# First block of a two-block transformer: output product, second norm, up and down products joined into one stage

## The reference, cut to what matters

```
mixed = sigmoid(g_ssm) * (y_ssm @ w_ssm_out) + sigmoid(g_att) * (y_att @ w_att_out)
h = h + mixed @ w_o                                   # output product, 1024 -> 1024
hn = rmsnorm(h, norm2_g)                              # second norm
a, b = hn @ w_up[:, :2816], hn @ w_up[:, 2816:]       # up product
c = a[t-2]*conv_w[0] + a[t-1]*conv_w[1] + a[t]*conv_w[2] + conv_b   # along the sequence
h = h + (gelu(c) * b) @ w_down                        # down product, 2816 -> 1024
return h[16:528]                                      # 512 tokens go on to the second block
```

## Time and profile before

| | us |
|---|---|
| median of the runs | 2160.52 |
| lowest and highest of 3 | 2160.28, 2163.2 |
| span of the profiled execution | 2159.5 |
| busy TensorE, VectorE, ScalarE in it | 1979.5, 1357.7, 955.4 |

### The profile page before, as it was taken

How to read it: one execution, slowest core, us unless ns; L and a number is a source line. 1 busy time by engine, 2 the same in 40 slices (tenths; PEclk the granted TensorE clock), 3 DMA queues, 4 the chain that set the end, 5 groups by cost and what they waited for, 6 DMA issues and landing times. The chain is left out here.

```text
span 2159.5 us, 29553 instructions
## 1 busy us (share of the span) xinstructions
PE 1979.5 (92%) x11864; PEld 1644.8 (76%) x11864; DVE 1357.7 (63%) x1895; ACT 955.4 (44%) x1409; POOL 163.7 (8%) x209
## 2 busy tenths in 40 slices
PE   5998997997999989899997999978998999799996
PEld 5888887996899978687675888866786667688884
DVE  7874543726455454443346999975526783799996
ACT  5562434402111000252445777752224884677773
POOL 3443000000000000000010200020000000110010
PEclk9999998997999999999998999997997999899998
DMA  7434111314223122232141999971531001299993
GB/s 218 103 82 111 61 40 59 116 45 88 97 79 110 67 78 80 84 98 78 40 147 53 361 401 396 377 269 35 156 114 51 21 21 59 89 382 400 385 384 139
DMA packets 176327, 322.37 MB, mean 149 GB/s; under 512 B 46736, under 2 KB 112976, under 8 KB 176192
## 3 DMA queue, kind: packets, MB, share of 16 engines
q1 hardware_dynamic: 148464, 282.92, 37.5%
q0 software_dynamic: 11488, 31.28, 4.5%
q10 hardware_dynamic: 16240, 6.29, 1.1%
HBM read 299.41 MB, written 17.89 MB: 147 GB/s over the span
## 5 line engine op out<-in xcount | busy, mean ns | idle before, releaser
L2318 PE MATMUL ps<-m_ws,m_xbT 128*128 128x512 f32 x1344 | 314.5, 390 | 0.0
L2318 PEld LDWEIGHTS ps<-m_ws,m_xbT 128*128 128x128 f32 x1344 | 251.9, 188 | 52.1
L2545 DVE TENSOR_TENSOR m_ws<-ring,m_ws 128x2048 fp32r<-128x2048 f32 x112 | 256.0, 2289 | 15.8 <-ACT m_ws L2394 14.3
L1648 PE MATMUL ps<-ffT,ff_ws 128*128 128x264 f32 (+1 forms) x1056 | 241.6, 324 | 4.4 <-DVE ff_ws L433 4.4
L2394 ACT CAST m_ws<-ring 128x2048 fp32r<-128x2048 f32 x112 | 212.9, 1907 | 42.4 <-PE ps L2360 24.8
L1648 PEld LDWEIGHTS ps<-ffT,ff_ws 128*128 128x128 f32 x1056 | 176.8, 190 | 20.2 <-DVE ff_ws L433 4.5
L1648 PE MATMUL ps<-ffT_lo,ff_ws 128*128 128x264 f32 (+1 forms) x528 | 170.3, 322 | 0.0
L2360 PE MATMUL ps<-m_ws,m_hT 128*128 128x512 f32 x672 | 167.3, 398 | 0.0
L2542 DVE TENSOR_TENSOR m_ws<-ring,m_ws 128x2048 fp32r<-128x2048 f32 x56 | 128.2, 2290 | 24.8 <-ACT m_ws L2392 24.8
L2360 PEld LDWEIGHTS ps<-m_ws,m_hT 128*128 128x128 f32 x672 | 122.2, 188 | 23.6
L2392 ACT CAST m_ws<-ring 128x2048 fp32r<-128x2048 f32 x56 | 107.0, 1910 | 51.4 <-PE ps L2318 30.7
(11 more groups left out here) (548 smaller groups left out, 4078.8 us busy)
## 6 DMA issues: line engine op xcount, KB each, us to landing
ring<-in_moe_w_gate SPq DMA_DIRECT2D x112, 512.0 KB, 5.7
ring<-in_moe_w_up SPq DMA_DIRECT2D x112, 512.0 KB, 8.1
ring<-in_moe_w_down SPq DMA_DIRECT2D x56, 1024.0 KB, 8.4
ring<-in_w_up SPq DMA_DIRECT2D x22, 1024.0 KB, 5.2
ring<-in_w_in SPq DMA_DIRECT2D x16, 1024.0 KB, 6.9
ring<-in_gla_w_in SPq DMA_DIRECT2D x12, 1024.0 KB, 5.3
ring<-in_w_down SPq DMA_DIRECT2D x11, 1024.0 KB, 4.8
ring<-in_nsa_w_in SPq DMA_DIRECT2D x10, 1024.0 KB, 11.0
```

The lines of the kernel that those rows point to most:

```text
L1648: ins = nc.tensor.matmul(ps[:, bank, 0:b - a], w[j][:, k, s * P:(s + 1) * P], x[l][:, k, a:b], start=(k == 0 and j == l), stop=(k == KD - ...
L2318: ins = nc.tensor.matmul(ps[:, it % 2, :], xbT[:, blk % 2, a, 4 * half + k, :].bitcast(F32R), v[b][:, k, :], start=(half == 0 and k == 0 a ...
L2545: ins = V.tensor_tensor(o, x.rearrange("p (j k w) -> p j k w", k=4, j=2), x0, ALU.subtract)
```

## The change

The five stages become one, `mix_stage`. The split of weight slabs there is done by `Split` throughout, ScalarE rounding and VectorE subtracting; `Split` now gets a list of places ("homes") and of the event that frees each, in place of a fixed number of buffers.

- **Output product by token tile.** For each of the five token tiles, the 16 learned tokens first, all four weight slabs are used in turn, so the four slabs have to stay resident (two of them in the memory of `qkT` and `gT`). A tile is finished after 4 x 24 matmuls. VectorE adds it at once to its row of `h`, ScalarE squares it, takes its own logarithm and exponential, VectorE scales it, and TensorE transposes it in the middle of the following tile's product (`turn_y`); the last tile is turned within the first up products.
- **Up product.** The `a` halves have 258 columns in place of 264 (the first 12 learned tokens aren't needed by the convolution). The first two turns are rearranged so that products on the first tiles run while the last tile is being normed. Each turn has a ScalarE rounding of a slab in place of the VectorE one.
- **Down product.** The first input pair is split while the up product still runs. The last two slabs are done by token tile: all 24 matmuls of a tile, then the next tile; a finished tile is added to `h` and transposed (`turn_x`) during the next tile's matmuls. The high and low parts go to buffers (`xT_hi`, `xT_lo`) that the GLA stage reads, and the stage `x0` is gone.
- **Loads.** The norm's and the convolution's weights are loaded by POOL after the reload of `x`, in place of ScalarE's queue at the start of two stages.

The core of the diff (lines that are only "..." leave parts out):

```diff
@@ output product, TensorE
-                for j in range(4):
-                    w = S.both(pe, 21 + j, slab_view(KD, 256))
-                    for b, (n, c0, t) in enumerate(KT):
-                        x = 5 * j + b
...
+                for x, (n, c0, t) in enumerate(KT):
+                    if x >= 2:
+                        pe.wait_ge(h_added, x - 1)
+                    for j in range(4):
+                        w = S.both(pe, 21 + j, slab_view(KD, 256))
...
+                        if j == 1 and x:
+                            turn_y(x - 1)
@@ second norm, ScalarE, for each tile
+                for x, (n, c0, t) in enumerate(KT):
+                    act.wait_ge(h_added, x + 1)
+                    if x >= 2:
+                        act.wait_ge(turned, 2 * (x - 1))
+                    link(nc.scalar.activation(y2[0:n, x % 2, :], h[0:n, t, :], ACT.Square, accum_out=st[0:n, 0, x:x + 1]))
+                    link(nc.scalar.activation(st[0:n, 1, x:x + 1], st[0:n, 0, x:x + 1], ACT.Ln, bias=eps[0:n], scale=1 / D))
+                    nc.scalar.activation(st[0:n, 2, x:x + 1], st[0:n, 1, x:x + 1], ACT.Exp, scale=-0.5).then_inc(rs, 1)
+                    for hf in range(2):
+                        act.wait_ge(turned, 2 * x + hf + 1)
+                        nc.scalar.copy(hT[:, 4 * hf:4 * hf + 4, c0:c0 + n].bitcast(F32R), turn_bank(x, hf, n)).then_inc(xt_hi, 1)
+                    if x == 3:
+                        F.hi(act, 1)
+                        F.hi(act, 2)
@@ up product, TensorE
+                up(0, 0, 2, 0, A_HALVES[0])
+                pe.wait_ge(h_added, NK)
+                up(0, 1, 0, 0, A_HALVES[0])
+                pe.wait_ge(xt_lo, 8)
+                up(1, 0, 6, 0, B_HALVES[0])
+                turn_y(NK - 1)
+                up(1, 1, 7, 0, B_HALVES[0])
+                pe.wait_ge(xt_lo, 10)
...
+                for i in range(2, FT):
+                    s = i % 2
+                    pe.wait_ge(a_out, i - 1)
+                    up(i // 2 * 2, s, 2 - 2 * s, 0, A_HALVES[0])
+                    up(i // 2 * 2, s, 3 - 2 * s, 0, A_HALVES[1], a_done)
+                    pe.wait_ge(g_done, i - 1)
+                    up(i // 2 * 2 + 1, s, 6 + s, 0, (META, T1), b_done)
@@ up product, VectorE (ScalarE's turns: copy of a, gelu, F.hi)
+                for it in range(FT + 1):
+                    if it:
+                        F.lo(dve, it + 2)
...
+                        V.tensor_tensor(glu(i)[:, 0], ge[:, i % 2], ps[:, 6 + i % 2, :], ALU.mult).then_inc(g_done, 1)
+                    if it == FT - 1:
+                        down_x(0)
@@ down product, TensorE
+                for i in range(ND - 2):
+                    for kk in range(2):
+                        for t in range(TT):
+                            if i == 0 and kk == 0 and t:
+                                pe.wait_ge(*((a_out, FT - 1), (a_out, FT), (g_done, FT))[t - 1])
+                            ins = down(i, kk, t)
+                    ins.then_inc(dn_read, 1)
+                for t in range(TT):
+                    for i in range(ND - 2, ND):
+                        for kk in range(2):
+                            ins = down(i, kk, t)
+                    ins.then_inc(y_done, 1)
+                    if t:
+                        turn_x(t - 1)
+                turn_x(TT - 1)
@@ second block
-                self.norm_stage("x0", TILES2, h, None, m["xh"], None, None, None, 0.0, dstT_lo=m["xl"])
```

More of the change, by code:

```diff
@@ L360, in weight_order @@
         self.n_moe.append(self.moe_slabs(1))
-    def fm_product(self, slab, kt, w, col, rhs, spans, done, m=P):
-        v = slab_view(kt, w)(self.W.slot(slab))
-        for bank, a, b in spans:
-            for k in range(kt):
-                ins = self.nc.tensor.matmul(self.ps[0:m, bank, 0:b - a], v[:, k, col:col + m], rhs(k, a, b),
-                                            start=(k == 0), stop=(k == kt - 1))
-        ins.then_inc(done, 1)
-        return ins
     def fm_product3(self, w, col, x, out, done, m=P):
@@ L508, in _ @@
-                if dstT is None:
-                    return
-                for i, (r, t, c0) in enumerate(tiles):
+                for t in range(TT if dstT is not None else 0):
                     for hf in range(2):
-                        act.wait_ge(turned, 2 * i + hf + 1)
-                        to = dstT[:, 4 * hf:4 * hf + 4, c0:c0 + r]
-                        nc.scalar.copy(to if dstT_lo is None else to.bitcast(F32R), banks(2 * i + hf, r)).then_inc(evac, 1)
+                        act.wait_ge(turned, 2 * t + hf + 1)
+                        nc.scalar.copy(dstT[:, 4 * hf:4 * hf + 4, P * t:P * (t + 1)].bitcast(F32R), bank(t, hf)).then_inc(evac, 1)
@@ L1499, in _, with up @@
                                                        start=(k == 0 and wa == xa), stop=(k == KD - 1 and xa == 1))
-                        ins.then_inc(o_done, 1)
+                        if j == 3:
+                            ins.then_inc(o_done, 1)
+                        elif x == NK - 1 and j < 2:
+                            ins.then_inc(o_read, 1)
+                        if j == 1 and x:
+                            turn_y(x - 1)
+                def up(q, s, bank, cols, span, done=None):
+                    w = F.both(pe, q, slab_view(KD, 256))
+                    a, b = span
+                    for k in range(KD):
+                        for wa, xa in THREE:
+                            ins = nc.tensor.matmul(ps[:, bank, cols:cols + b - a], w[wa][:, k, s * P:(s + 1) * P], (hT, hlo)[xa][:, k, a:b].bitcast(F32R),
+                                                   start=(k == 0 and wa == xa), stop=(k == KD - 1 and wa == 1))
+                    if done is not None:
+                        ins.then_inc(done, 1)
@@ L1559, in _ @@
                 V.memset(eps[:], EPS).then_inc(start, 1)
+                link(V.memset(st[:], 0.0))
                 def rest(lo, x, hi):
@@ L1619, in _ @@
+                for hf in range(2):
+                    rest_x(TT - 1, hf)
             @block.sync
@@ L3291, in build @@
         K = Program(nc, A, places1, places2, root)
-        K.first_block(stop)
-        if stop not in ("n1", "s5", "mix", "first"):
-            K.second_block(out, stop)
-        if stop:
-            with nc.Block() as block:
-                @block.sync
-                def _(sp):
-                    for n in range(K.W.sent - RING, K.W.sent):
-                        K.W.arrived(sp, n)
+        ctx = root.enter_context(ExitStack())
+        held = Held(ctx, *(ctx.enter_context(nc.sbuf_tensor(n, [P, KD, T1], F32, side="right")) for n in ("xT_hi", "xT_lo")))
+        K.first_block(held.x)
+        K.second_block(out, held)
 def kernel(**inputs):
```

600 lines of the change are left out of this document (258 added, 342 removed).

## The result

The changed kernel takes 2139.97 us (median of 4 runs, 2138.2 to 2141.5) beside 2161.45 for the kernel before on the same chips; the ratio is 0.9901, with a 95% interval of 0.9887 to 0.9915. It is faster by 21.5 us; 30.9 were forecast. The time lies at the upper end of the 2121 to 2140 that the prediction gave for 8 in 10, and outside the 2125 to 2134 of the forecast itself. The profiled execution has a span of 2139.6 us.

A forecast was written before the change was run, and what follows sets the result against it. TensorE, busy 92% of the span, was taken as the bound. Terms -23.6 + 5.8 - 2.6 - 7.9 - 2.6 = -30.9 against 2159.5 gave 2128.6, with 1.0 us added 2129.6; forecast itself 2125 to 2134, 8-in-10 range 2121 to 2140.

The forecast's parts named there:

- Term 1: Between output and up product: the norm's 25.1 us pause and 2.7 us go, transposes cost 4.2; -23.6 us.
- Term 2: Output product: transposes wait 1.4 to 1.5 us for the norm's chain with two table loads, at four tiles; +5.8 us.
- terms 1 to 3: Output and up products: norm's pause gone (-23.6 us), new wait for the norm's chain (+5.8), narrower matmuls (-2.7).
- Term 3: Up product: 6 columns less in each of 1056 matmuls; -2.7 us, at worst 0; split `b` products give back 0.1.
- Term 4: Into the down product: 6.7 us pause and 2.1 us slow clock go, a new wait costs 0.9; -7.9 us.
- The wait that the term did name: Down product's fourth token tile waits for banks freed by the last multiplication by `b`, behind a slab's low part; +0.9 us.
- Term 5: Way into the second block (GLA stage): transposes between down matmuls and a shorter way, 7.6 for 10.2 us; -2.6 us.
- The low clock under the 16-token tile: Rival, start of output product: 16-column weights keep the clock at half; +7 us, 2137; chance 0.16.
- if they wake the clock gate: Output product: transposes' waits for the norm might lower the clock, costing about as much as the +7 us rival (chance 0.16).
- bound by the vector engines: Rival, up product: chained ScalarE and VectorE work makes turns 13 us, so slower than before, 2165; chance 0.04.
- the dear table switch: Rival, norm's chain in output product: each load delays twice over, TensorE waits 4.0 us at four tiles; 2140 to 2148; chance 0.07.

The follow-up runs named there:

- the first experiment: Changed kernel with one table set for logarithm and exponential, loaded once ahead of the norm's loop in place of two loads per tile: 2133.94 us, ratio 0.9879.

## Why the prediction was right and wrong

- **Term 1** held: the up product follows the output product with no pause.
- **Term 2** had the mechanism right and the size too small: four waits of 1.3 us (forecast 1.4 to 1.5), with two loads of 1.28 in front, which the first experiment shows to be the cause. But it cost 7.4 us and not 5.8, chiefly since the clock fell behind the first wait (1.3 us). The prediction had such a fall only in a rival. This 1.6 is what terms 1 to 3 lack together. The activation starts 0.01 us after its load, and the chain grew by 2.56 us for two loads. So the drain that the Trainium skill (ScalarE: Activation LUTs, section "What ACT_TABLE_LOAD costs") adds is not seen. The Trainium skill (ScalarE: Activation LUTs, section "Table sets: the hidden batching unit") says that one set holds both functions. That is true in the run that loads it by name; the changed kernel loads twice all the same.

```profile
455.06 1.28 ACT L1544 ACT_TABLE_LOAD   x1
456.35 0.30 ACT L1544 ACTIVATE n_st<-n_st,mx_eps 128x1 f32<-128x1 f32 x1
456.67 1.28 ACT L1545 ACT_TABLE_LOAD   x1
457.96 0.20 ACT L1545 ACTIVATE n_st<-n_st 128x1 f32<-128x1 f32 x1
```

- **Term 3** held: 11.30 us a turn.
- **Term 4** is the step that failed: -7.9 forecast, -0.3 measured (743.3 to 873.1 less 1.6 of transposes is 128.2 us, for 128.5 from 763.1 to 891.6). "The 6.7 us pause goes; its input pair and slab are split during the up product" took it that what is issued early enough is done early enough. The pair's low part is issued in the last turn but one and stood behind that turn's slab, the last convolution and a multiplication: 3.63 us. The wait that the term did name was 3.00 and not 0.9, hidden behind this. "2.1 us of slow clock after the pause go too" failed with it: 1.5 came back. And 10.88 us a slab were taken over, although the buffers of both operands were new: 3.2 us.
- **Term 5** came out near its number (-2.3 for -2.6) by luck, since two errors met: 1.2 us of transposes too many between the down matmuls, and a way into the GLA stage 1.5 us too short. "the way into the GLA stage, 1.1 us as now" was read from a boundary with a plain barrier, 0.35 us on VectorE. The clearing of semaphores, which stood one boundary earlier, is now at this one: 1.3 us.
- **Behind it** 2.5 of the 22.4 us by which the GLA stage starts earlier were lost again in the profiled executions. The GLA stage's first products took 7.95 us for 6.66, at a clock of 0.79 for 1.00; all its weight products together span 253.0 for 253.3, so that is given back. But the first expert product stands 38.8 us behind them for 37.6, the first expert stage took 284.7 for 283.4, and the rest 0.3 more. Over all variants these two were 37.6 to 39.0 and 281.3 to 285.9, and no run was made on them: why stays open.
- **The rivals.** The low clock under the 16-token tile did not come: it was 0.71 in 428 to 430, for 0.73 before, and 1.00 in 430 to 432. Waits of term 2 "if they wake the clock gate" did so once (below). Up turns were never bound by the vector engines. The 2140 of the dear table switch and the 2137 of the low clock are near the measured 2139.97 by accident: neither mechanism occurred.

## What to carry to other kernels

When stages are merged, go through each engine's issue order at the seam, instruction by instruction, and ask for each input not when its data is there but what stands in front of the instruction that makes it; and when one such wait is removed, look for the next one close behind it, since the first edit may show no gain alone, as here. A matmul's pace belongs to its buffers' places as well as to its shape: after moving either operand, measure it anew. What stands at a boundary (barriers, clearing, loads behind them) moves to the next boundary when a stage disappears.

## What was not expected of the hardware

- **Distance of a matmul's operands.** With 128x512 matmuls on fp32 data in steady flow, 48 of them take 10.88 us when stationary and moving operand start at the same remainder of 512 bytes. They took 11.19 or 11.20 when the remainders differed by 32, 128 or 224 bytes, and 10.98 when they differed by 192; both operands moved by 32 bytes alike, 10.88 again. The differences are worked out from the sizes of the tiles in the kernels, not read from a trace. (In the changed kernel they are those of the odd inputs; the even inputs' two parts lie at different remainders.) Which modulus is the true one was not settled; 512 is enough.
- **Short waits and the clock.** The first of the four waits of 1.3 us was followed by half clock; the other three were not. In front of the first stood 5.7 us of products with 128 stationary columns and before these the 16-token tile with its 16 columns, and right behind it the eight 16x16 transposes of that tile. Around the others all was of full size. Without the wait the same order kept its clock (last row, the run with one table set). Which of the narrow matmuls matters was not tested.

```profile
444.00:446.00 2.00, 1.46 (x15) 1.44 (x16) 0.93 (x3) 0.42 (x2) 0.00 (x0) 1.00 0.00 0
446.00:448.00 2.00, 2.00 (x12) 2.00 (x12) 0.00 (x0) 0.00 (x0) 0.00 (x0) 0.55 0.00 0
448.00:450.00 2.00, 2.00 (x13) 2.00 (x12) 0.00 (x0) 0.00 (x0) 0.00 (x0) 0.59 0.00 0
450.00:452.00 2.00, 2.00 (x19) 2.00 (x19) 0.00 (x0) 0.00 (x0) 0.00 (x0) 1.00 0.03 8
...
446.00:448.00 2.00, 2.00 (x19) 2.00 (x19) 0.00 (x0) 0.00 (x0) 0.00 (x0) 1.00 0.00 0
```

  Its price: the adds on either side are 14.96 us apart, the others 13.7.
- **The same pause can cost differently:** that of 3.6 us ahead of the down product cost some 1.5 us of slow clock in one kernel and 2.7 in another. Why was not tested.
